# Block products for nine pairs of expert tiles in the second half of the V product

## The chip, the cores and the metric

The kernel runs on one core of one Trainium2 chip. Its time is the device time of one launch in microseconds (us); it is given as the median of several runs. One execution was taken with the hardware profiler, and every duration below comes from that execution.

## The reference

The kernel computes two transformer blocks in a row for 256 tokens of width 2048 in float32. The last step of the second block is a mixture of 16384 small experts (`peer_ffn`), and it is the only part that the change touches:

```
u = u_emb[expert]
a = jax.nn.gelu(jnp.einsum('thkd,td->thk', u, xb), approximate=False)
coef = (g * a)
return jnp.einsum('thk,thkd->td', coef, v_emb[expert])
```

`expert` holds 8 x 16 chosen experts for each token, and `g` their softmax weights. The result is added to the residual stream, and a last rmsnorm with the gain `g_final` gives the output, 256 x 2048.

## The kernel before

**Dense form.** Instead of gathering experts, the kernel makes a dense table of coefficients, 16384 experts x 256 tokens, zero where a token did not choose an expert. It lies in SBUF as `G`, 128 tiles of 128 experts x 256 tokens. The result is then a plain matrix product: for each expert tile j, coefficients (128 x 256 tokens) times rows of V (128 experts x 2048 columns), summed over j.

**Three products for one.** A float32 operand is split into a high part (`wh`, the value rounded to the narrow format fp32r) and a low part (`wl`, the remainder). TensorE computes high x high, high x low and low x high; that is `three` (lines 941 to 943). So one block product is three matmuls of 128 x 512.

**Two halves.** V is worked through twice: first columns 0 to 1023 for all 128 tiles ("first half"), then columns 1024 to 2047 ("second half"). One tile of a half is one chunk of 128 x 1024 floats, 512 KB. For each chunk `v_part_of` runs four block products (2 token blocks x 2 column blocks of 512), 12 matmuls, into four PSUM banks that accumulate over j: banks `ps4` to `ps7` in the first half and `ps0` to `ps3` in the second (`acc`).

**The engines around one chunk.** All chunks of the program stand in one list, `PLAN`.
- SP loads chunk i into one of four raw buffers (`load`, line 842), once VectorE has finished with chunk i-4 (semaphore `lo`). SP also issues every other DMA, in program order.
- ScalarE makes the high part (`cut`, line 2273), once TensorE has finished chunk i-3, and the high part of the coefficients of the next tile (`coef_high`, line 2655) into one of two buffers, once TensorE has finished the tile that used that buffer.
- VectorE makes the low parts (`coef_low`, line 2189, which counts the semaphore `c_l`; `cut`, line 1481, which counts `lo`).
- In the loop over j of the second half, ScalarE runs in turn `coef_high` for tile j+1 and `cut` for tile j+2, and VectorE runs `coef_low` for tile j+1 and `cut` for tile j+2, while TensorE works on tile j. "Step j" below means that turn.

**Other work in the second half.** The residual stream was parked in DRAM (`spill`). As tiles of `G` are used up, their space takes the residual (`fin`) and the gain (`gain`), in twelve pieces of 256 KB (`PIECE`, lines 918 and 920). Before piece n SP waits until `c_l` says that the tiles under it have been read (`c_l` at least 128 + 2n + 2, that is, the coefficients of tile 2n+1), and each stands in SP's order ahead of the load of tile 10 + 2n. At steps 50 to 62 VectorE adds the finished first half to the residual (`add_up`, line 2207), ScalarE squares it (line 2671) and VectorE multiplies by the gain (line 2236). After the last matmul the second half is added, the norm is taken and the output is stored.

Of the kernel before, what the change touches and what calls it, by code (L numbers as in the profile page):

```python
# [16 lines left out]
D = 2048  # L17
# [143 lines left out]
PLAN += [("V", j, c) for c in range(2) for j in range(128)]  # L161
# [333 lines left out]
def build(nc, A, out):  # L495
# [184 lines left out]
    fin = flatG[:, 0:2 * D].rearrange("p (q d) -> p q d", q=2)  # L680
# [26 lines left out]
    def pc(name, i=0):  # L707
# [53 lines left out]
        new(n) for n in ("v_part", "f_add", "f_sq", "f_ms", "f_rt", "f_rs", "f_out", "f_outv")]  # L761
    block = top.enter_context(nc.Block())
# [74 lines left out]
    def _(y):  # L837
# [42 lines left out]
        for i in range(RN, NCH):  # L880
# [58 lines left out]
    def _(t):  # L939
# [495 lines left out]

        def v_last():
# [16 lines left out]
        for i in range(U0, NCH):  # L1453
            name, j, c = PLAN[i]
            if name == "U":
                if c == 0:
                    if j < 4:
                        t.wait_ge(qp_ok, 5 + j)
                    else:
                        t.wait_ge(ev_u, j - 3)  # L1460
                chunk(i, u_place(j), 8 * c, 8, x4, c == 0, c == 1)
            elif (j, c) == (125, 1):
                v_last()
            elif c == 0 or j < 125:
                v_tile(j, c)
# [6 lines left out]
    def _(v):  # L1472
# [731 lines left out]
        def add_up(half, qt, b):  # L2204
            i = 2 * half + b
            x = fin[:, qt, 512 * i:512 * i + 512]
            v.tensor_tensor(x, x, acc(half, qt, b)[:], ALU.add).then_inc(f_add, 1)

        for j in range(128):
            if j < 125:  # L2210
# [12 lines left out]
            else:  # L2223
                cut(V1 + j + 2)
            if j in ADD_AT:
                n = ADD_AT.index(j)
                if n == 0:
                    v.wait_ge(d_re, 16 * 8)
                add_up(0, n // 2, n % 2)
            if j - 2 in ADD_AT:  # L2230
                n = ADD_AT.index(j - 2)
                if n == 0:
                    v.wait_ge(d_gf, 16 * 4)
                x = fin[:, n // 2, 512 * (n % 2):512 * (n % 2) + 512]
                v.wait_ge(f_sq, n + 1)
                v.tensor_tensor(x, x, gain[:, 512 * (n % 2):512 * (n % 2) + 512], ALU.mult).then_inc(own.up(), 1)
        for qt in range(2):
            for b in range(2):
# [18 lines left out]
            for c in (CH, CH + 512):  # L2257
                y = fin[:, qt, c:c + 512]
# [4 lines left out]
    def _(s):  # L2263
# [661 lines left out]
```

## Time and profile before

| | |
|---|---|
| median of 3 runs | 3174.89 us (3174.85 to 3175.99) |
| profiled execution | 3175.95 us |
| its span, first to last instruction | 3174.1 us |
| TensorE busy | 3160.3 us |
| VectorE busy | 2096.0 us (66%) |
| ScalarE busy | 1804.0 us (57%) |
| DMA, mean over the span | 198 GB/s |

Busy times are sums of the durations of instructions. Matmuls are pipelined and overlap in the records: one is shown as 389 ns although the next starts sooner. How long a piece of TensorE work takes is therefore read from start to start. On VectorE and ScalarE, too, an instruction may start a little before the record of the one ahead of it ends. The granted clock of TensorE is given as a share of full speed: 1.00 is 2.4 GHz, 0.50 is 1.2 GHz.

### The profile page before, as it was taken

To read this page: it belongs to the slowest core of one execution; us is meant where nothing else is said; L and a number is where in the kernel's file an instruction comes from. 1 tells how busy PE (TensorE), PEld (TensorE's weight loads), DVE (VectorE), ACT (ScalarE), POOL (GpSimd) and SP (SyncE) were. 2 spreads that over 40 slices of the span, in tenths; PEclk is the share of its full clock that TensorE was granted. 3 is DMA by queue.
4 is the path that set the end of the run, shared out by engine and by line. 5 is a ranking of instruction groups with operands and counts; after the bars stand their busy time and mean duration, and the time that the engine had idled before them with its cause. 6 is when DMAs were issued, how large, how long until landed. Compare 5 with 4: busy or idle time off the path is not lost.

```text
span 3174.1 us, 58774 instructions
## 1 busy us (share of the span) xinstructions
PE 3160.3 (100%) x24186; PEld 3018.3 (95%) x24186; DVE 2096.0 (66%) x3389; ACT 1804.0 (57%) x2580; POOL 458.0 (14%) x321
## 2 busy tenths in 40 slices
PE   9999999999999999999999999999999999999998
PEld 9999999999999999999999999999999888888887
DVE  7987486666664477665666699855555666666665
ACT  6566464444444455545455578877777544555545
POOL 0001200000000000000000056777760000000000
PEclk9999999999999999999999999999999999999999
DMA  6444557666666656545565577888876777766555
GB/s 224 151 146 134 183 181 235 225 226 229 226 201 194 194 172 206 163 153 166 187 196 197 199 190 194 196 195 195 194 195 196 243 242 242 242 226 216 195 194 168
DMA packets 229419, 627.77 MB, mean 198 GB/s; under 512 B 59328, under 2 KB 78624, under 8 KB 229024
## 3 DMA queue, kind: packets, MB, share of 16 engines
q1 hardware_dynamic: 192144, 623.60, 60.7%
q0 software_dynamic: 36864, 0.15, 3.3%
q8 instruction: 192, 3.15, 0.4%
q14 instruction: 75, 0.61, 0.1%
q10 hardware_dynamic: 144, 0.26, 0.0%
HBM read 601.27 MB, written 21.10 MB: 196 GB/s over the span
## 4 chain that ended last, share of the span: by engine, by line
PE 98%; DVE 1%; ACT 0%; DMA 0%; issue 0%; POOL 0%; SPq 0%; DVEq 0%; ACTq 0%; POOLq 0%
PE ps L941 32%; PE ps L942 31%; PE ps L943 31%; PE ps L1014 0%; DVE wl L1481 0%; PE ps L1215 0%; PE ps L1238 0%; PE ps L1235 0%; PE ps L982 0%; DMA raw<-in_in1k 0%; PE ps L1411 0%; PE ps L1249 0%; PE ps L1239 0%; PE ps L1067 0%; PE ps L1016 0%
## 5 line engine op out<-in xcount | busy, mean ns | idle before, releaser
L2273 ACT CAST wh<-raw 128x1024 fp32r<-128x1024 f32 (+3 forms) x1114 | 1158.2, 1040 | 1029.7 <-PE ps L943 1008.4
L1481 DVE TENSOR_TENSOR wl<-raw,wh 128x1024 fp32r<-128x1024 f32 (+2 forms) x883 | 1061.8, 1203 | 407.8 <-ACT wh L2273 405.4
L941 PE MATMUL ps<-xh,wh 128*128 128x256 f32 x3088 | 854.7, 277 | 0.5 <-issue 0.5
L943 PE MATMUL ps<-xh,wl 128*128 128x256 f32 x3088 | 850.0, 275 | 0.0
L942 PE MATMUL ps<-xl,wh 128*128 128x256 f32 x3088 | 849.8, 275 | 0.0
L941 PE MATMUL ps<-xw,wh 128*128 128x258 f32 (+2 forms) x2096 | 591.7, 282 | 2.8 <-DVE wl L1542 1.7
L943 PE MATMUL ps<-xw,wl 128*128 128x258 f32 (+2 forms) x2096 | 587.6, 280 | 0.0
L941 PEld LDWEIGHTS ps<-xh,wh 128*128 128x128 f32 x3088 | 579.7, 188 | 4.3 <-issue 1.6
L942 PEld LDWEIGHTS ps<-xl,wh 128*128 128x128 f32 x3088 | 579.8, 188 | 1.1 <-issue 1.0
L943 PEld LDWEIGHTS ps<-xh,wl 128*128 128x128 f32 x3088 | 579.6, 188 | 0.0
L2784 POOL DMA_INDIRECT table<-w_loose x256 | 397.6, 1553 | 809.3 <-DVE w_loose L2161 656.3
L1481 DVE TENSOR_TENSOR wl<-raw,ph 128x1024 fp32r<-128x1024 f32 x231 | 281.2, 1220 | 224.4 <-ACT ph L2278 187.7
L942 PE MATMUL ps<-xw,wh 128*128 128x258 f32 (+2 forms) x1441 | 404.2, 281 | 0.0
L941 PEld LDWEIGHTS ps<-xw,wh 128*128 128x128 f32 x2096 | 394.3, 188 | 5.4 <-DVE wl L1542 2.1
L943 PE MATMUL ps<-wh,coefs 128*128 128x512 f32 x1020 | 396.8, 389 | 0.0
L941 PE MATMUL ps<-wh,coefs 128*128 128x512 f32 x1020 | 396.8, 389 | 0.0
L942 PE MATMUL ps<-wl,coefs 128*128 128x512 f32 x1020 | 396.8, 389 | 0.0
L943 PEld LDWEIGHTS ps<-xw,wl 128*128 128x128 f32 x2096 | 394.0, 188 | 0.0
L942 PEld LDWEIGHTS ps<-xw,wh 128*128 128x128 f32 x1441 | 270.8, 188 | 0.1
L2278 ACT CAST ph<-raw 128x1024 fp32r<-128x1024 f32 x231 | 232.7, 1007 | 0.0
L941 PEld LDWEIGHTS ps<-wh,coefs 128*128 128x128 f32 x1020 | 191.4, 188 | 39.8
L943 PEld LDWEIGHTS ps<-wh,coefs 128*128 128x128 f32 x1020 | 191.4, 188 | 39.8
(398 smaller groups left out, 4454.7 us busy)
## 6 DMA issues: line engine op xcount, KB each, us to landing
raw<-in_peer_u SPq DMA_DIRECT2D x256, 512.0 KB
raw<-in_peer_v SPq DMA_DIRECT2D x256, 512.0 KB
raw<-in_w_in SPq DMA_DIRECT2D x172, 512.0 KB
raw<-in_w_up SPq DMA_DIRECT2D x82, 512.0 KB
raw<-in_w_gate SPq DMA_DIRECT2D x80, 512.0 KB
raw<-in_w_down SPq DMA_DIRECT2D x80, 512.0 KB
raw<-in_w_out SPq DMA_DIRECT2D x64, 512.0 KB
table<-tmp SPq DMA_DIRECT2D x32, 512.0 KB, 6.4
```

Source lines behind the costliest of these rows:

```text
L941: t.matmul(o, lh, rh, start=start, stop=False)
L942: t.matmul(o, lh, rl, start=False, stop=False)
L943: return t.matmul(o, ll, rh, start=False, stop=stop)
L1481: v.tensor_tensor(part_at(wl, i), raw[:, i % RN, 0:cols(i)], high.bitcast(F32), ALU.subtract).then_inc(lo, 1)
L2273: last = s.copy(part_at(wh, i), raw[:, i % RN, 0:cols(i)])
L2278: last = s.copy(ph[:, 2 + i % 2, :], raw[:, i % RN, 0:cols(i)])
L2784: g.indirect_dma_start(out=table, out_offset=bass.IndirectOffsetOnAxis(ap=eidx[q][:, n:n + 1], axis=0), in_=wts[q][:, n:n + 1], in_offset= ...
```

## The change

Nine pairs of neighbouring tiles, (26, 27), (36, 37), ... (106, 107), are taken out of the normal course of the second half. For a pair the product is a 2 x 2 by 2 x 2 product of blocks (2 token blocks, 2 expert tiles, 2 column blocks), and Strassen's scheme gives it with seven block products in place of eight, some of them of sums of blocks.

- **TensorE** (`v_pair`): seven products of three matmuls for a pair instead of eight. They go to seven banks: three of the usual four (`ps0`, `ps1`, `ps2`) and `ps4` to `ps7`, which must be free by then. So the first half is added to the residual at steps 11 to 14 now, no longer at 50 to 62.
- **VectorE and ScalarE** (`pair_step`): in the eight steps ahead of a pair, eight sums on VectorE (four of 128 x 512, four of 128 x 128), then the high part of 4096 columns on ScalarE and the low part on VectorE, in five pieces each. The two `cut`s of the pair's tiles fall away. A new pair's sums begin when TensorE has finished the pair before.
- **SP**: a pair's two raw tiles are loaded by two DMAs of 512 KB of their own (line 961 of the changed kernel) into the space of `G` under the old `fin`, ahead of the load that is named in `PAIR_LOAD`. For the first pair that is the load of tile 20; for the others it is the load of the first tile behind the pair before (tile 28, 38, ...), and SP first waits until VectorE has made the second low piece of the pair before (`pair_lo`), because that piece reads the same space.
- **Pieces**: the twelve pieces of residual and gain now stand ahead of the loads of tiles 8, 10, 12, 14 (residual, first half), 109 to 112 (residual, second half) and 18, 20, 22, 24 (gain). Their numbers n, and with them the count of `c_l` that SP waits for, are 0 to 3, 4 to 7 and 8 to 11 in that order.
- **Fold**: behind the last pair one copy and eight adds of 128 x 512 bring `ps4` to `ps7` into the residual, at steps 108 to 116.

```diff
+PAIRS = [26 + 10 * n for n in range(9)]
+PAIRED = [j + e for j in PAIRS for e in range(2)]
+SINGLE = [j for j in range(128) if j not in PAIRED]
+PLAN += [("V", j, 0) for j in range(128)] + [("V", j, 1) for j in SINGLE]
...
-PIECE = {AT["V", 10 + 2 * n, 1]: n for n in range(12)}
-
-ADD_AT = [50 + 4 * n for n in range(4)]
+PIECE = {AT["V", j, 1]: n for n, j in enumerate((8, 10, 12, 14, 109, 110, 111, 112, 18, 20, 22, 24))}
+
+ADD_AT = [11, 12, 13, 14]
+SQUARE_AT, GAIN_AT = [54, 64, 74, 84], [55, 65, 75, 85]
+
+
+BETWEEN = PAIRS[1] - PAIRS[0] - 2
+PAIR_LOAD = {AT["V", 20, 1]: 0}
+PAIR_LOAD.update({AT["V", j - BETWEEN, 1] + 8: n + 1 for n, j in enumerate(PAIRS[:-1])})
+BEHIND_PAIR = {j - BETWEEN + o: (n, o) for n, j in enumerate(PAIRS) for o in range(BETWEEN)}
+FOLD = {PAIRS[-1] + 3 + n: n for n in range(8)}
...
+    def fin_at(qt, c, n=512):
+        o = 2 * CH * (c // CH) + CH * qt + c % CH
+        return flatG[:, o:o + n]
+    pair_high, pair_low = [x[:, PAD_X[3]:PAD_X[3] + KT * S] for x in xbuf]
+    pair_raw = x_loose[:, 1, PAD_X[3]:PAD_X[3] + KT * S]
+    B11, B21, B22, T1_, T3_, T2_, T4_, SUMS = range(8)
+    RAW11, RAW12, RAW21, RAW22 = [flatG[:, 2 * CH + 512 * n:2 * CH + 512 * n + 512] for n in range(4)]
+    RAW_ROWS = flatG[:, 3 * CH:4 * CH]
+    folded = flatG[:, 3 * D + 3 * CH:3 * D + 3 * CH + 512]
...
                 y.wait_ge(c_l, 128 + 2 * n + 2)
                 c = slice(512 * (n % 4), 512 * (n % 4) + 512)
+                if n == 4:
+                    y.wait_ge(pair_lo, PAIR_LO + 5 * (len(PAIRS) - 1) + 2)
                 if n < 8:
-                    y.dma_start(fin[:, n // 4, c], spill[:, n // 4, c]).then_inc(d_re, 16)
+                    qt, x = n // 2 % 2, CH * (n // 4) + 512 * (n % 2)
+                    y.dma_start(fin_at(qt, x), spill[:, qt, x:x + 512]).then_inc(d_re if n < 4 else d_gf, 16)
                 else:
                     y.dma_start(gain[:, c], A["g_final"][:, c]).then_inc(d_gf, 16)
+            if i in PAIR_LOAD:
+                n = PAIR_LOAD[i]
+                if n:
+                    y.wait_ge(pair_lo, PAIR_LO + 5 * (n - 1) + 2)
+                else:
+                    y.wait_ge(c_l, 128 + 16)
+                for e in range(2):
+                    j = PAIRS[n] + e
+                    y.dma_start(flatG[:, (2 + e) * CH:(3 + e) * CH], A["peer_v_2"][128 * j:128 * j + 128, CH:2 * CH]).then_inc(d_pair, 16)
             load(i)
...
+        def v_pair(n):
...
+            t.wait_ge(pair_lo, PAIR_LO + 5 * (n + 1))
+            t.wait_ge(c_l, one + 1)
+            product(ps[4], single(one, 0), B11, first, last)
+            product(ps[5], summed(0), T1_, first, last)
+            t.wait_ge(c_l, two + 1)
+            product(acc(1, 0, 0), single(two, 0), B21, False, False)
+            product(acc(1, 1, 0), single(two, 1), T4_, False, False).then_inc(pair_mm, 1)
+            product(acc(1, 0, 1), summed(3), B22, False, False)
+            product(ps[6], summed(1), T2_, first, last)
+            product(ps[7], summed(2), T3_, first, last).then_inc(pair_mm, 1)
...
+                if c and j - 2 in PAIRS:
+                    v_pair(PAIRS.index(j - 2))
                 v_tile(j, c)
...
+            done = PAIR_SUM + 8 * n
+            if o == 0:
+                if n:
+                    v.wait_ge(pair_mm, PAIR_MM + 2 * n)
+                v.wait_ge(d_pair, D_PAIR + 32 * (n + 1))
+                v.tensor_tensor(t1, RAW12, RAW11, ALU.subtract).then_inc(pair_sum, 1)
+                v.tensor_tensor(t3, RAW22, RAW12, ALU.subtract).then_inc(pair_sum, 1)
+                v.tensor_tensor(sums[0], a21, a22, ALU.add).then_inc(pair_sum, 1)
+                v.wait_ge(pair_sum, done + 1)
+                v.tensor_tensor(t2, RAW22, t1, ALU.subtract).then_inc(pair_sum, 1)
+            elif o == 1:
+                v.wait_ge(pair_sum, done + 3)
+                v.tensor_tensor(sums[1], sums[0], a11, ALU.subtract).then_inc(pair_sum, 1)
+                v.wait_ge(pair_sum, done + 4)
+                v.tensor_tensor(t4, RAW21, t2, ALU.subtract).then_inc(pair_sum, 1)
+            elif o == 2:
+                v.tensor_tensor(sums[2], a11, a21, ALU.subtract).then_inc(pair_sum, 1)
+                v.wait_ge(pair_sum, done + 5)
+                v.tensor_tensor(sums[3], a12, sums[1], ALU.subtract).then_inc(pair_sum, 1)
+            if 2 <= o < 7:
+                pair_low_of(n, o - 2)
+
+        def pair_low_of(n, q):
+            x, y = ((0, 512), (512, 1536), (1536, 2560), (2560, 3584), (3584, 4096))[q]
+            whole_ = RAW11 if q == 0 else RAW_ROWS if q == 1 else pair_raw[:, x:y]
+            v.wait_ge(pair_hi, PAIR_HI + 5 * n + q + 1)
+            v.tensor_tensor(pair_low[:, x:y], whole_, pair_high[:, x:y].bitcast(F32), ALU.subtract).then_inc(pair_lo, 1)
...
+            steps = [(folded, ps[4]), (fin_at(0, CH + 512), folded), (fin_at(0, CH + 512), ps[5]), (folded, ps[7]),
+                     (fin_at(1, CH), folded), (fin_at(1, CH + 512), folded), (fin_at(1, CH + 512), ps[5]), (fin_at(0, CH), ps[4])]
...
+            if j in PAIRS:
+                coef_low(128 + j + 1)
+                cut(AT["V", j + 2, 1] + 2)
+                continue
...
+            elif n >= 130 and n - 130 in PAIRED:
+                s.wait_ge(pair_mm, PAIR_MM + 2 * (PAIRED.index(n - 130) // 2) + 1)
...
+        def pair_step(n, o):
+            if o > 4:
+                return
+            x, y = ((0, 512), (512, 1536), (1536, 2560), (2560, 3584), (3584, 4096))[o]
+            whole_ = RAW11 if o == 0 else RAW_ROWS if o == 1 else pair_raw[:, x:y]
+            if o == 0:
+                if n:
+                    s.wait_ge(pair_mm, PAIR_MM + 2 * n)
+                s.wait_ge(d_pair, D_PAIR + 32 * (n + 1))
+            elif o > 1:
+                s.wait_ge(pair_sum, PAIR_SUM + 8 * n + (2, 6, 8)[o - 2])
+            s.copy(pair_high[:, x:y], whole_).then_inc(pair_hi, 1)
```

**SP, second half of V, the loads of tiles 14 to 30.** `raw<-in_peer_v` is a chunk's load, `G<-spill` and `G<-in_g_final` are pieces of residual and gain, `G<-in_peer_v` is a raw tile of a pair; `s_c_l`, `s_lo` are the semaphores that SP waits for. Before:

```order
L842 DMA raw<-in_peer_v_2 128x1024 [waits s_lo] x2
L918 DMA G<-spill 128x512 [waits s_c_l]
L842 DMA raw<-in_peer_v_2 128x1024 [waits s_lo] x2
L918 DMA G<-spill 128x512 [waits s_c_l]
L842 DMA raw<-in_peer_v_2 128x1024 [waits s_lo] x2
L918 DMA G<-spill 128x512 [waits s_c_l]
```

And after:

```order
L871 DMA raw<-in_peer_v_2 128x1024 [waits s_lo] x4
L952 DMA G<-in_g_final 128x512 [waits s_c_l]
L871 DMA raw<-in_peer_v_2 128x1024 [waits s_lo] x2
L952 DMA G<-in_g_final 128x512 [waits s_c_l]
L961 DMA G<-in_peer_v_2 128x1024 [waits s_c_l]
L961 DMA G<-in_peer_v_2 128x1024
L871 DMA raw<-in_peer_v_2 128x1024 [waits s_lo] x2
L952 DMA G<-in_g_final 128x512 [waits s_c_l]
L871 DMA raw<-in_peer_v_2 128x1024 [waits s_lo] x2
L952 DMA G<-in_g_final 128x512 [waits s_c_l]
L871 DMA raw<-in_peer_v_2 128x1024 [waits s_lo] x2
L961 DMA G<-in_peer_v_2 128x1024 [waits s_cv_l]
```

The gain's four pieces, which stood ahead of tiles 26 to 32, stand ahead of tiles 18, 20, 22 and 24, each with a wait for `c_l`, and the first pair's raw tiles stand between the second of them and the load of tile 20.

**VectorE, steps 18 to 20 of the second half.** `coefs` is the low part of coefficients, `wl` that of a chunk, `x_loose` the place of a pair's sums, `xl` and `xh` a pair's low and high part. Before:

```order
L2189 TENSOR_TENSOR coefs<-G,coefs 128x256 [waits s_c_h]
L1481 TENSOR_TENSOR wl<-raw,wh 128x1024 [waits s_hi]
L2189 TENSOR_TENSOR coefs<-G,coefs 128x256 [waits s_c_h]
L1481 TENSOR_TENSOR wl<-raw,wh 128x1024 [waits s_hi]
L2189 TENSOR_TENSOR coefs<-G,coefs 128x256 [waits s_c_h]
```

And after:

```order
L1552 TENSOR_TENSOR wl<-raw,wh 128x1024 [waits s_hi]
L2290 TENSOR_TENSOR x_loose<-G 128x512 [waits s_d_km]
L2291 TENSOR_TENSOR x_loose<-G 128x512
L2292 TENSOR_TENSOR x_loose<-G 128x128
L2294 TENSOR_TENSOR x_loose<-G,x_loose 128x512 [waits s_cv_add]
L2260 TENSOR_TENSOR coefs<-G,coefs 128x256 [waits s_c_h]
L1552 TENSOR_TENSOR wl<-raw,wh 128x1024 [waits s_hi]
L2297 TENSOR_TENSOR x_loose<-x_loose,G 128x128 [waits s_cv_add]
L2299 TENSOR_TENSOR x_loose<-G,x_loose 128x512 [waits s_cv_add]
L2260 TENSOR_TENSOR coefs<-G,coefs 128x256 [waits s_c_h]
```

Four sums now stand between the `cut` of step 18 and the coefficients of tile 20, and two between the `cut` of step 19 and the coefficients of tile 21.

## Rows read from the trace of the kernel before

**Rows 1.** The page: engines, and the chain that ended last by engine.

```profile
PE 3160.3 (100%) x24186; PEld 3018.3 (95%) x24186; DVE 2096.0 (66%) x3389; ACT 1804.0 (57%) x2580; POOL 458.0 (14%) x321
...
PE 98%; DVE 1%; ACT 0%; DMA 0%; issue 0%; POOL 0%; SPq 0%; DVEq 0%; ACTq 0%; POOLq 0%
```

**Rows 2.** Waits, 2900 to 3100 us: engine line waited for, us, times, longest.

```profile
ACT coefs L2655 <- PE ps L943: 96.7, 73, 1.4
DVE wl L1481 <- ACT wh L2273: 39.1, 74, 0.5
DVE coefs L2189 <- ACT coefs L2655: 35.7, 66, 0.5
```

**Rows 3.** Timeline around one tile's start: start, us, engine, line, operation.

```profile
3002.16 0.39 PE L943 MATMUL ps<-wh,coefs 128*128 128x512 f32 x1
3002.38 0.39 PE L941 MATMUL ps<-wh,coefs 128*128 128x512 f32 x1
3002.58 0.41 ACT L2655 CAST coefs<-G 128x256 fp32r<-128x256 f32 x1 [1.36 <-PE ps L943]
3002.89 1.05 ACT L2273 CAST wh<-raw 128x1024 fp32r<-128x1024 f32 x1
3003.02 0.42 DVE L2189 TENSOR_TENSOR coefs<-G,coefs 128x256 fp32r<-128x256 f32 x1 [0.54 <-ACT coefs L2655]
3003.97 1.23 DVE L1481 TENSOR_TENSOR wl<-raw,wh 128x1024 fp32r<-128x1024 f32 x1 [0.53 <-ACT wh L2273]
3005.30 0.41 ACT L2655 CAST coefs<-G 128x256 fp32r<-128x256 f32 x1 [1.36 <-PE ps L943]
```

**Rows 4.** Timeline of VectorE with an add behind a cut, and of ScalarE near the end.

```profile
2955.01 1.23 DVE L1481 TENSOR_TENSOR wl<-raw,wh 128x1024 fp32r<-128x1024 f32 x1 [0.53 <-ACT wh L2273]
2956.16 0.68 DVE L2207 TENSOR_TENSOR G<-G,ps 128x512 f32<-128x512 f32 x1
2956.78 0.43 DVE L2189 TENSOR_TENSOR coefs<-G,coefs 128x256 fp32r<-128x256 f32 x1
...
3157.93 0.62 ACT L2683 CAST wh<-raw 128x512 fp32r<-128x512 f32 x1
3158.46 0.61 ACT L2684 CAST wh<-raw 128x512 fp32r<-128x512 f32 x1
```

**Rows 5.** Timeline of SP's queue, tiles 10 to 18 of the second half.

```profile
2831.15 3.05 SPq L842 DMA_DIRECT2D raw<-in_peer_v  x2
2834.24 0.43 SPq L918 DMA_DIRECT2D G<-spill  x1
...
2852.91 3.05 SPq L842 DMA_DIRECT2D raw<-in_peer_v  x2
```

**Rows 6.** Transfers of 256 KB: line 920 alone, and the page's DMA issues.

```profile
L920 SPq DMA_DIRECT2D G<-in_g_final x4: 432/432/432, 2872.3 to 2888.6; - x4
...
DMA to landing us min/median/max: 4.4/4.9/5.4
...
out<-G SPq DMA_DIRECT2D x7, 256.0 KB, 2.7
```

**Rows 7.** Stretches: busy us of PE, PEld, DVE, ACT, POOL; PEclk, DMA share, GB/s.

```profile
2999.79:3000.79 1.00, 1.00 (x6) 0.81 (x5) 0.43 (x1) 0.93 (x2) 0.00 (x0) 1.00 0.38 115
3000.79:3003.19 2.40, 2.40 (x12) 2.00 (x11) 1.40 (x2) 1.04 (x3) 0.00 (x0) 1.00 0.58 203
3003.19:3003.39 0.20, 0.20 (x3) 0.16 (x2) 0.20 (x1) 0.20 (x1) 0.00 (x0) 1.00 0.15 61
10.00:24.00 14.00, 13.96 (x112) 13.96 (x113) 11.49 (x17) 12.06 (x20) 2.02 (x7) 1.00 1.01 382
```

**Rows 8.** Timeline: the last matmul of the program.

```profile
3165.55 0.40 PE L943 MATMUL ps<-wh,xl 128*128 128x512 f32 x1
```

**Rows 9.** Stretches behind the last matmul.

```profile
3167.00:3168.00 1.00, 0.00 (x0) 0.00 (x0) 0.30 (x2) 0.64 (x4) 0.00 (x0) 1.00 1.05 352
3168.00:3168.50 0.50, 0.00 (x0) 0.00 (x0) 0.20 (x3) 0.22 (x2) 0.00 (x0) 0.83 0.96 336
3168.50:3169.00 0.50, 0.00 (x0) 0.00 (x0) 0.50 (x1) 0.50 (x1) 0.00 (x0) 0.50 0.13 45
```

**Rows 10.** Waits of TensorE over the whole span, the longest kinds.

```profile
PE ps L941 <- DVE wl L1542: 1.7, 2, 1.2
PE ps L941 <- issue: 1.6, 2, 1.1
```

More of the change, by code:

```diff
@@ L1434, in v_tile, with product, single, summed @@
             last.then_inc(gemm, 1)
+        def v_pair(n):
+            j = PAIRS[n]
+            one, two = 128 + j, 128 + j + 1
+            first, last = n == 0, n == len(PAIRS) - 1
+            def product(o, left, b, start, stop):
+                return three(o[:], *left, pair_block(pair_high, b), pair_block(pair_low, b), start, stop)
+            def single(tile, qt):
+                tk = slice(128 * qt, 128 * qt + 128)
+                return coef_at(0, tile)[:, tk], coef_at(1, tile)[:, tk]
+            def summed(i):
+                return pair_sum_at(pair_high, i), pair_sum_at(pair_low, i)
+            if first:
+                t.wait_ge(f_add, 4)
+            t.wait_ge(pair_lo, PAIR_LO + 5 * (n + 1))
[8 more added lines that the diff above has]
+            product(ps[7], summed(2), T3_, first, last).then_inc(pair_mm, 1)
         def v_last():
@@ new lines, in pair_low_of, with fold @@
+        def pair_low_of(n, q):
[3 more added lines that the diff above has]
+            v.tensor_tensor(pair_low[:, x:y], whole_, pair_high[:, x:y].bitcast(F32), ALU.subtract).then_inc(pair_lo, 1)
+        def fold(n):
+            steps = [(folded, ps[4]), (fin_at(0, CH + 512), folded), (fin_at(0, CH + 512), ps[5]), (folded, ps[7]),
+                     (fin_at(1, CH), folded), (fin_at(1, CH + 512), folded), (fin_at(1, CH + 512), ps[5]), (fin_at(0, CH), ps[4])]
+            x, y = steps[n]
+            if n == 0:
+                v.wait_ge(pair_hi, PAIR_HI + 5 * len(PAIRS) + 1)
+                v.wait_ge(d_gf, 16 * 8)
+            else:
+                v.wait_ge(pair_sum, PAIR_SUM + 8 * len(PAIRS) + n)
+            v.tensor_tensor(x, x, y if y is folded else y[:], ALU.add).then_inc(pair_sum, 1)
@@ L2222, in _ @@
                 last.then_inc(lo, 1)
-            else:
-                cut(V1 + j + 2)
+            elif j in SINGLE and j - 2 not in PAIRS:
+                cut(AT["V", j, 1] + 2)
+            if j in BEHIND_PAIR:
+                pair_step(*BEHIND_PAIR[j])
+            if j in FOLD:
+                fold(FOLD[j])
             if j in ADD_AT:
@@ L2684, in _ @@
                 s.copy(part_at(wh, i)[:, 512:CH], raw[:, i % RN, 512:CH]).then_inc(hi, 1)
-            else:
+            elif j in SINGLE and j - 2 not in PAIRS:
                 cut(AT["V", j, 1] + 2)
-            if j - 1 in ADD_AT:
-                n = ADD_AT.index(j - 1)
+            if j in BEHIND_PAIR:
+                pair_step(*BEHIND_PAIR[j])
+            if j == PAIRS[-1] + 2:
+                s.wait_ge(pair_mm, PAIR_MM + 2 * len(PAIRS))
+                s.copy(folded, ps[6][:]).then_inc(pair_hi, 1)
+            if j in SQUARE_AT:
+                n = SQUARE_AT.index(j)
                 square_up(0, n // 2, n % 2)
@@ L2708, in _ @@
                 s.wait_ge(f_out, 4)
-                s.dma_start(out[128:256, 512:1024], fin[:, 1, 512:1024]).then_inc(d_out, 16)
+                s.dma_start(out[128:256, 512:1024], fin_at(1, 512)).then_inc(d_out, 16)
     @block.gpsimd
```

39 lines of the change are left out of this document (26 added, 13 removed).

## The prediction

> **What bounds the kernel now.** I read the page first, then the waits, then the timeline of one tile, then SP's queue and the transfers. The page shows TensorE busy for the whole span and 98% of the chain on it [rows 1]; over the whole span its longest wait is 1.2 us [rows 10]. In the second half of V every other engine waits: ScalarE 1.36 us in each tile for TensorE, VectorE twice 0.54 us for ScalarE [rows 2, 3]. So a matmul taken away is time gained, as long as nothing makes TensorE wait; and a delay elsewhere costs only what exceeds its slack.
>
> A tile takes 2.72 us (3002.58 to 3005.30) and is 12 matmuls, 0.227 us each [rows 3]. From its start (3002.38) its ScalarE copy begins after 0.20 us, and the low coefficients for the next tile are ready after 1.06 us (3003.44).
>
> What an instruction takes of its engine, start to start: on VectorE a 1024-column cut 1.15 us (2955.01 to 2956.16), a 512-column add 0.62 [rows 4], coefficients 0.34 (0.43 less the overlap of 0.09 seen on the others); a 128-column sum I extrapolate from 0.43 at 256 and 0.68 at 512 columns to 0.29, so 0.2 start to start. On ScalarE coefficients 0.31 [rows 3], 512 columns 0.53 [rows 4], 1024 columns 1.05 less 0.09, 0.96.
>
> **Part 1, the matmuls removed.** Nine pairs, three matmuls less in each: 27 x 0.227 = 6.1 us saved. It is the same form (128 x 512) from other buffers, so I take the same 0.227.
>
> **Part 2, the work added on VectorE and ScalarE.** In ten tiles, now 8 x 2.72 + 21 x 0.227 = 26.5 us of TensorE, VectorE has 10 coefficients (3.4), 8 cuts (9.2), six instructions of 512 columns (3.7), three of 1024 (3.4) and four small ones (0.8): 20.5 us, 77%. ScalarE has 3.1 + 7.7 + 1.1 + 2.9 = 14.8 us. Both fit in the mean. What hides this work is VectorE's idle time of 2 x 0.54 us a tile [rows 3]; without the overlap of 0.09 us on 31 instructions it would be 23.3 us, still less than 26.5. I cost it at nothing in the course between pairs. The fold's nine instructions (8 x 0.62 us on VectorE, one a step) fall in steps with 1.1 us of idle time and without pair work: nothing, at most 5 us if none were hidden. The adds of the first half come earlier; their four pieces are ordered six steps ahead. Nothing. The end of the kernel is unchanged.
>
> **Part 3, SP's queue from tile 18 to 25.** This is the term that decides. Before, the piece ahead of tile 18's load had n = 4 and asked for the coefficients of tile 9; the load was out at 2852.91 [rows 5], step 13 of this half. Now the piece there has n = 8, so SP waits for c_l = 128 + 18, the coefficients of **tile 17**, which VectorE makes in step 16. In the same step ScalarE wants tile 18's raw data. Behind the waiting instruction stand the load of tile 18, that of tile 19, and the next piece, which wants tile 19's coefficients, and so on four times (tiles 18, 20, 22, 24). The four loads in advance shrink to none.
>
> Price of a landing: a 512 KB load issued at 2999.79 moves little before 3000.79 and is mostly done by 3003.39, 3.6 us after issue [rows 7]; 256 KB take 2.7 us alone, and 4.9 us behind a 512 KB load that was issued 0.4 us earlier [rows 6]. Under a full queue 382 GB/s are moved [rows 7], 1.37 us for 512 KB. From the first and second I take 2.3 us + 1.45 us for each 512 KB queued in one burst; bounds are 2.0 + 1.3 (2.7 us less 0.7; the full queue) and 3.1 + 1.6 (5.3 us from the load's issue for 768 KB, less 1.5 units; 3.6 us less 2.0).
>
> The chain, in us from the start of tile 16:
> - Coefficients 17 at 1.06, SP issues gain and load 18 (1.5 units, 4.5 us): landed 5.6. ScalarE high part to 6.65, VectorE low part 7.9, coefficients 18 behind it 8.2, tile 18 starts at 8.3. It was due at 5.44: **2.9 late**.
> - Load 19 lands at 7.0, its high part is done at 8.1 and its low part at 9.4; coefficients 19 at 9.7. Now gain, the pair's 1 MB and load 20 go out together, 3.5 units, 7.4 us: landed 17.1. High part 18.2, low part 19.4, four sums 3 x 0.62 + 0.2 ahead of coefficients 20, which end at 21.85. Tile 20 starts at 21.9, while tile 19 ended at 13.75: **8.2 late**.
> - Low part 21 (1.15), two sums (0.8), coefficients 21 at 24.15. Gain and load 22, 4.5 us: 28.65. High 29.75, low 31.0, two small sums and a piece of 512 columns 1.0, coefficients 22 at 32.35. Tile 22 at 32.45, due 27.4: **5.1 late**.
> - Low part 23, a pair piece of 1024 columns (both 1.15), coefficients 23 at 35.0. Load 24 landed 39.5, high 40.55, low 41.8, pair piece 1.15, coefficients 24 at 43.3. Tile 24 at 43.4, due 37.9: **5.5 late**.
>
> Sum 21.7 us. With the lower bounds it is 19.2, with the upper 26.1, by the same chain.
>
> **Part 4, a pair's raw tiles ahead of a load.** For the other pairs SP waits for the second low piece of the pair before. In us from the start of the first tile behind a pair: that piece comes in the fourth step and ends at 12.1. The pair's two tiles and the load of the first tile behind the pair are 3 units, 2.3 + 4.35: landed 18.8. ScalarE wants it in the seventh step, at 16.8. So its high part is done at 19.85, its low part at 21.1, then the last low piece of the pair (0.68) at 21.7 and the pair's coefficients at 22.1; the pair is due at 21.76. 0.4 late, and 0.12 at the pair's second tile: 0.52 x 7 = 3.6 us (the pair at 26 falls in part 3, the one at 106 has no load in its way). By the bounds it is nothing (landed 17.9) or 1.8 each, 13 us.
>
> **Part 5, the clock.** The last matmul starts at 3165.55 [rows 8], the granted clock is still 1.00 up to 3168.0 and 0.50 from 3168.5 on, which is 1.2 GHz [rows 9]. The stalls of 8.2, 5.1 and 5.5 us are longer than that gap. At half speed a matmul costs 0.2 us more. The first two slow starts hide in the next stall, where ScalarE's and SP's chain decides; only the last one counts. How fast the clock comes back no row of before shows: between nothing and one whole tile (2.4 us); I take the middle, 1.2.
>
> The Trainium skill (TensorE: Matmul & The Clock Gate, section "HAM oscillation — how this bites in real kernels") says that a kernel whose matmuls stop for each DMA wait starts each batch at the low clock. The trace agrees as far as it can, with the fall to 0.50 behind the last matmul. By that rule part 5 would be above nothing, and without it nothing.
>
> **The sum.** 21.7 + 3.6 + 1.2 - 6.1 = 20.4 us. The profiled execution took 3175.95 us (span 3174.1), so it would take 3196.4; the median of the runs is 1.1 lower: **3195 us**.
>
> On the price of a landing the Trainium skill (DMA: Bandwidth & Descriptors, section "Anatomy of one DMA — SWDGE (gpsimd) path") fits 2.0 us + bytes / 436 GB/s for another issuing path. That would be 1.2 us for each 512 KB, and the sum by it, an estimate, some 12 us slower than before. The rows here show more (3.6 us for one load, 382 GB/s), and I keep to them.
>
> **Rivals.**
> - *Quick landings.* The lower bounds in parts 3 and 4: 19.2 + 0 + 1.2 - 6.1 = +14.3 us, 3189. For it speaks 382 GB/s under load; against it the 4.9 us of a gain piece behind one load.
> - *Slow landings, and pairs that wait each time.* The upper bounds: 26.1 + 13 + 1.2 - 6.1 = +34, 3209. For it speaks that at 1000 columns a step VectorE has little room in the steps with pair pieces, so that part 4's delay is not made up; against it that a single load is done in 3.6 us.
> - *SP's wait stays covered (the other side).* Then only the 27 matmuls count: 3168.8, or up to 3172 with part 4. It would decide if the load of tile 18 landed before 3.0 us in the chain above, so that its low part were ready at 5.4: within 1.9 us of its issue. The shortest 256 KB transfer, 2.7 us [rows 6], speaks against it. For it speaks only that none of the twelve piece waits of before delayed anything, but there the tile asked for was nine tiles ahead of the load behind it, and now it is one.
> - *VectorE as the bound of the whole half*: were its instructions not to overlap and the waits for its own results to add 0.1 us each, the steps with pair pieces would take some 3 us instead of 2.72, 1.5 us a pair at most, 13 us. It is held by the upper end.
>
> **How the numbers follow.** My forecast (between +17 and +27 us) 0.55; quick landings 0.17; slow landings or VectorE 0.21; covered wait 0.06; anything else 0.01. A measurement of this kernel can tell 0.2%, 6.3 us, from no change; the covered wait ends just inside it, at -6.1, and by a little more or less on either side of it: 0.02 of its 0.06 for faster, 0.04 for the same, and another 0.01 for the same from what is not thought of. So faster 0.02, same 0.05, slower 0.93. The range, 3185 to 3211, takes in both landing bounds.
>
> **What would show it.** Right: in the profile after, TensorE waits four times near tiles 18, 20, 22 and 24, the second time longest, some 22 us in all, for coefficients or cuts whose ScalarE copy waited for a DMA; the granted clock falls there; SP's loads of 18 to 25 come in twos. Then 27 matmuls fewer, and 0 to 1 us of waiting ahead of each pair. Wrong: no wait of TensorE ahead of tile 18 (then the load did not hang on the coefficients of tile 17), a matmul of a pair that takes more than 0.227 us, or VectorE without idle time from tile 28 on.

## The result

The changed kernel takes 3209.09 us (median of 4 runs, 3208.24 to 3210.67) against 3174.88 us: the ratio is 1.0107, 95% interval 1.009 to 1.0125, that is 34.2 us slower. The forecast was 3195 us in a range of 3185 to 3211. The time is in the range and near its upper end, so the sum was 14 us too small.

### The profile page after: what moved, and what is told of

The parts are those of the page before. It is cut to its first block, busy times and chain, and to the rows that moved or that the text cites. A ratio compares the mean times of both kernels' runs of the same rounds, so it can differ in the third digit from the quotient of the medians.

```text
span 3206.4 us, 58846 instructions
## 1 busy us (share of the span) xinstructions
PE 3172.4 (99%) x24159; PEld 3018.8 (94%) x24159; DVE 2142.9 (67%) x3496; ACT 1821.8 (57%) x2608; POOL 459.2 (14%) x321
## 4 chain that ended last, share of the span: by engine, by line
PE 95%; DVE 2%; DMA 2%; ACT 1%; issue 0%; SPq 0%; POOL 0%; DVEq 0%; ACTq 0%; POOLq 0%
PE ps L982 31%; PE ps L983 30%; PE ps L984 30%; DMA raw<-in_peer_v 1%; DVE wl L1552 1%; PE ps L1055 0%; ACT wh L2397 0%; DVE xl L2311 0%; PE ps L1256 0%; PE ps L1279 0%; PE ps L1276 0%; PE ps L1023 0%; PE ps L1452 0%; DVE coefs L2260 0%; PE ps L1290 0%
## 5 line engine op out<-in xcount | busy, mean ns | idle before, releaser
L2397 ACT CAST wh<-raw 128x1024 fp32r<-128x1024 f32 (+3 forms) x1096 | 1138.9, 1039 | 1074.7 <-PE ps L984 1014.6
L1552 DVE TENSOR_TENSOR wl<-raw,wh 128x1024 fp32r<-128x1024 f32 (+2 forms) x865 | 1039.8, 1203 | 415.8 <-ACT wh L2397 411.5
L982 PE MATMUL ps<-wh,coefs 128*128 128x512 f32 x948 | 375.1, 396 | 18.8 <-DVE coefs L2260 18.8
L983 PE MATMUL ps<-wl,coefs 128*128 128x512 f32 x948 | 373.5, 394 | 0.0
L984 PE MATMUL ps<-wh,coefs 128*128 128x512 f32 x948 | 373.4, 394 | 0.0
L982 PEld LDWEIGHTS ps<-wh,coefs 128*128 128x128 f32 x948 | 179.8, 190 | 58.8 <-issue 16.2
L984 PEld LDWEIGHTS ps<-wh,coefs 128*128 128x128 f32 x948 | 180.8, 191 | 39.9
```

Of the source, the lines that this page charges most:

```text
L982: t.matmul(o, lh, rh, start=start, stop=False)
L983: t.matmul(o, lh, rl, start=False, stop=False)
L984: return t.matmul(o, ll, rh, start=False, stop=stop)
L1552: v.tensor_tensor(part_at(wl, i), raw[:, i % RN, 0:cols(i)], high.bitcast(F32), ALU.subtract).then_inc(lo, 1)
L2397: last = s.copy(part_at(wh, i), raw[:, i % RN, 0:cols(i)])
```

## The profile after

The page of the changed kernel, to be held against [rows 1]:

```profile
PE 3172.4 (99%) x24159; PEld 3018.8 (94%) x24159; DVE 2142.9 (67%) x3496; ACT 1821.8 (57%) x2608; POOL 459.2 (14%) x321
...
PE 95%; DVE 2%; DMA 2%; ACT 1%; issue 0%; SPq 0%; POOL 0%; DVEq 0%; ACTq 0%; POOLq 0%
```

27 matmuls are gone (24186 to 24159). The chain, 98% TensorE before, now has VectorE, DMA and ScalarE in it. The waits of the second half (2810 to 3200 us), engine and line, what it waited for, us, times, longest:

```profile
ACT wh L2397 <- DMA raw<-in_peer_v: 45.8, 13, 9.4
...
PE ps L982 <- DVE coefs L2260: 20.2, 8, 6.6
```

[rows 2] had no wait for a DMA at all. SP's own waits, before (2830 to 2880 us) and after (2855 to 2905 us):

```profile
SPq L842 <- DVE wl L1481: 38.5, 18, 2.4
...
SPq L952 <- DVE coefs L2260: 42.5, 4, 12.3
```

Before, SP waited for a free raw buffer, 2.4 us at most; now it waits four times, up to 12.3 us, for VectorE's low coefficients, in front of the gain's pieces. SP's queue, to be held against [rows 5], start and us:

```profile
2861.70 0.33 SPq L952 DMA_DIRECT2D G<-in_g_final  x1
2862.07 0.91 SPq L871 DMA_DIRECT2D raw<-in_peer_v  x2
2871.41 0.33 SPq L952 DMA_DIRECT2D G<-in_g_final  x1
2871.78 0.91 SPq L961 DMA_DIRECT2D G<-in_peer_v  x2
2872.73 1.14 SPq L871 DMA_DIRECT2D raw<-in_peer_v  x2
2886.22 0.33 SPq L952 DMA_DIRECT2D G<-in_g_final  x1
2886.59 0.91 SPq L871 DMA_DIRECT2D raw<-in_peer_v  x2
2897.72 0.33 SPq L952 DMA_DIRECT2D G<-in_g_final  x1
```

The loads of tiles 18 to 25 go out in twos, each two behind a gain piece, 9.7, 14.8 and 11.5 us apart where two tiles take 5.4. Step 16 begins at 2860.6, and the first gain piece goes out 1.1 us later, as the prediction's chain has it. ScalarE, which wants those loads:

```profile
2867.27 1.04 ACT L2397 CAST wh<-raw 128x1024 fp32r<-128x1024 f32 x1 [6.06 <-DMA raw<-in_peer_v]
2879.27 1.04 ACT L2397 CAST wh<-raw 128x1024 fp32r<-128x1024 f32 x1 [9.40 <-DMA raw<-in_peer_v]
2891.44 1.05 ACT L2397 CAST wh<-raw 128x1024 fp32r<-128x1024 f32 x1 [8.10 <-DMA raw<-in_peer_v]
2903.48 1.04 ACT L2397 CAST wh<-raw 128x1024 fp32r<-128x1024 f32 x1 [7.54 <-DMA raw<-in_peer_v]
```

From the gain piece's issue to the cut that waits for the load behind it: 5.6, 7.9, 5.2 and 5.8 us, where I had 4.5, 7.4, 4.5 and 4.5. TensorE at tiles 18, 20, 22 and 24 (the time in brackets is the idle time behind the end of the record ahead):

```profile
2870.05 0.47 PE L982 MATMUL ps<-wh,coefs 128*128 128x512 f32 x1 [3.85 <-DVE coefs L2260]
2884.06 0.76 PE L982 MATMUL ps<-wh,coefs 128*128 128x512 f32 x1 [6.63 <-DVE coefs L2260]
2895.23 0.76 PE L982 MATMUL ps<-wh,coefs 128*128 128x512 f32 x1 [3.44 <-DVE coefs L2260]
2907.41 0.77 PE L982 MATMUL ps<-wh,coefs 128*128 128x512 f32 x1 [4.88 <-DVE coefs L2260]
```

Tile 24 was due 21.8 us behind 2860.6, at 2882.4, and starts at 2907.4: 25.0 us late. From stall to stall, with the slow clock in between, TensorE lost 4.0, 8.6, 5.7 and 6.7 us. The clock, in stretches cut at its changes (columns as in [rows 7]; the eighth number is the granted clock):

```profile
2871.16:2874.57 3.41, 3.41 (x10) 2.64 (x9) 0.22 (x1) 0.00 (x0) 0.00 (x0) 0.50 0.53 102
2874.57:2881.40 6.83, 2.86 (x13) 2.00 (x11) 1.05 (x1) 2.13 (x4) 0.00 (x0) 1.00 0.77 294
2881.40:2888.23 6.83, 4.17 (x10) 3.33 (x11) 4.79 (x10) 1.94 (x3) 0.00 (x0) 0.50 0.13 23
...
2905.29:2912.12 6.83, 4.71 (x11) 3.78 (x12) 6.31 (x8) 2.36 (x4) 0.00 (x0) 0.50 0.93 362
2912.12:2940.00 27.88, 27.88 (x121) 22.55 (x121) 19.61 (x29) 15.50 (x23) 0.00 (x0) 1.00 0.45 156
```

It fell to 0.50 (1.2 GHz) within or just behind each of the four stalls. The matmuls between 2907.41 and 2912.12 started 0.427 us apart, 0.2 more than at 2.4 GHz, and the first two 0.56: 2.3 us in all.

The last stretch holds what I had not expected: 121 matmuls in 27.88 us with the clock at 1.00 and no wait, 0.230 us each, not 0.227. On a long stretch, 190 us, of before:

```profile
2960.00:3150.00 190.00, 190.00 (x840) 157.34 (x839) 119.03 (x147) 96.78 (x147) 0.00 (x0) 1.00 0.59 194
```

and of after:

```profile
2960.00:3150.00 190.00, 188.36 (x801) 149.99 (x800) 143.84 (x210) 106.16 (x163) 0.00 (x0) 1.00 0.56 193
```

The waits at pairs and the slow matmuls behind them take 3.8 us of this stretch, 16 or 17 of the missing 39 matmuls; the others are missing without a wait. From start to start plain tiles' matmuls go every 0.2333 us up to 3191, and every 0.2267 before 2865. I call these the slower and the faster rhythm.

So the 32.3 us by which the span is longer (3206.4 against 3174.1), with the last matmul starting at 3197.7 and not 3165.5, are made of: tile 24 late 25.0; half clock behind it 2.3; pairs waiting, with slow first matmuls, 3.9; some 1180 matmuls x 0.0066 = 7.8; less 6.1 for the 27 matmuls. That is 32.9; tile 16 started 0.3 us earlier than before, and the last 30 matmuls, as the next lines show, were 0.2 us quicker.

The slower rhythm is in the kernel before too, at its very end. There a weight load (PEld) starts 0.05 us behind the matmul ahead of its own:

```profile
3158.55 0.39 PE L943 MATMUL ps<-wh,coefs 128*128 128x512 f32 x1
3158.60 0.19 PEld L941 LDWEIGHTS ps<-wh,coefs 128*128 128x128 f32 x1
3158.78 0.39 PE L941 MATMUL ps<-wh,coefs 128*128 128x512 f32 x1
```

Up to there matmuls start 0.2267 us apart, and the last 30 start 0.23 and soon 0.2333 us apart. In the changed kernel the same place, at 3191, turns 0.2333 into 0.2267.

## The experiments

**Taking the held queue away.** `a1_gain_later`:

```diff
-PIECE = {AT["V", j, 1]: n for n, j in enumerate((8, 10, 12, 14, 109, 110, 111, 112, 18, 20, 22, 24))}
+PIECE = {AT["V", j, 1]: n for n, j in enumerate((8, 10, 12, 14, 109, 110, 111, 112, 30, 32, 34, 40))}
```

> The changed kernel with one edit: the gain's four pieces stand ahead of the loads of tiles 30, 32, 34 and 40 instead of 18, 20, 22 and 24, so that the coefficients they ask for are long made. Theory A (SP's queue, held by those waits, made the stalls of 4.2, 7.0, 3.8 and 5.3 us): no wait of TensorE from tile 18 to 25 and no fall of the clock; the stalls of 0.3 to 0.5 us ahead of pairs stay, about 3 us in all. Rival R (the pair's work itself, on ScalarE and VectorE, makes them): stalls stay near tiles 20 to 24. On the second thing seen after the change, that a matmul starts every 0.233 us instead of 0.227 from tile 24 on: theory M (a weight load that came late once puts TensorE into the slower rhythm, and it stays there) expects 0.233 us from the first stall ahead of a pair on, so 3174.9 - 6.1 + 3 + about 7.5 = 3179 us. Rival C (the slower rhythm comes from the clock's fall and return) expects 0.227 throughout and 3172 us.

Measured: 3184.47 us, ratio 1.0025 (1.0015 to 1.0036). 24.6 us of the 34.2 are gone with the place of four small DMAs; no wait is left at tiles 18 to 25, the clock stays at 1.00, and rival R falls. The time is 5 us above the 3179 us of theory M: the waits at pairs, with the slow matmuls behind them, came to 8.8 us and not 3. The first of them (1.4 us late from start to start):

```profile
2889.69 0.47 PE L982 MATMUL ps<-xh,coefs 128*128 128x512 f32 x1 [1.25 <-DVE coefs L2260]
```

The slower rhythm is there though the clock never fell, so rival C falls too. It began at tile 20, where nothing waited.

**The pairs' raw tiles.** `a2_pair_loads_later` is a1 with

```diff
-PAIR_LOAD.update({AT["V", j - BETWEEN, 1] + 8: n + 1 for n, j in enumerate(PAIRS[:-1])})
+PAIR_LOAD.update({AT["V", j - BETWEEN, 1] + 10: n + 1 for n, j in enumerate(PAIRS[:-1])})
```

> As the one before, and each pair's two raw tiles (but the first pair's) are loaded two loads later, ahead of the third single tile behind the pair before instead of the first. Theory A with part 4 of the prediction (the pair's 1 MB delayed the load behind it): no wait of TensorE at all in the second half, and with theory M or C alike 0.227 us a matmul: 3174.9 - 6.1 = 3168.8 us. Rival V (VectorE's work ahead of a pair makes the small stalls): they stay, 3172 to 3179 us. Rival F (matmuls that read a pair's buffers are slower by themselves): 0.233 us in or behind pairs without any stall, 3170 to 3177 us.

Measured: 3176.87 us, ratio 1.0004 (0.9995 to 1.0014). TensorE waits nowhere in the second half: the pairs' waits hang on the place of their raw loads, as part 4 says, and rival V falls. But the time is 8 us above 3168.8; the rhythm is the slower one from tile 20 on, as in a1. The timeline of a2 there (PEld is the weight load, which the engine begins one matmul ahead):

```profile
2870.46 0.42 DVE L2260 TENSOR_TENSOR coefs<-G,coefs 128x256 fp32r<-128x256 f32 x1
...
2870.71 0.39 PE L983 MATMUL ps<-wl,coefs 128*128 128x512 f32 x1
2870.71 0.19 PEld L984 LDWEIGHTS ps<-wh,coefs 128*128 128x128 f32 x1
...
2870.93 0.40 PE L984 MATMUL ps<-wh,coefs 128*128 128x512 f32 x1
2871.00 0.19 PEld L982 LDWEIGHTS ps<-wh,coefs 128*128 128x128 f32 x1
2871.17 0.39 PE L982 MATMUL ps<-wh,coefs 128*128 128x512 f32 x1
```

Each weight load starts with the matmul ahead of its own, until the one of tile 20: it starts 0.07 us behind. VectorE's four sums of step 18 had pushed the coefficients to 2870.88, 0.29 us ahead of the tile's first matmul but too late for its load. That matmul still starts on time. From there on the rhythm is 0.2333 us.

**The held queue alone.** `b1_hold_only` is the kernel before with

```diff
-PIECE = {AT["V", 10 + 2 * n, 1]: n for n in range(12)}
+PIECE = {AT["V", j, 1]: n for n, j in enumerate((10, 12, 14, 16, 26, 28, 30, 32, 18, 20, 22, 24))}
```

> The kernel before with one edit: the gain's four pieces stand ahead of the loads of tiles 18, 20, 22 and 24, where the changed kernel has them, and the residual's second four take their former places. No pairs. Theory A: four stalls of TensorE of 3.5 to 4 us at tiles 18, 20, 22 and 24, about 15 us, about 1 to 2 us of matmuls at half clock. Theory M or C adds 0.0067 us x 12 x 100 tiles = 8 us of slower rhythm behind them: 3200 us. If the held queue costs only what the new 1 MB and the pair's sums add: under 3180 us.

Measured: 3200.27 us, ratio 1.008 (1.0063 to 1.0097). Its waits from 2860 to 2905 us:

```profile
ACT wh L2273 <- DMA raw<-in_peer_v: 26.8, 5, 7.7
...
PE ps L941 <- DVE coefs L2189: 11.6, 4, 3.9
```

Without a single pair the new order of eight small DMAs costs 25 us, four stalls and the slower rhythm behind them. A piece of the same size stood ahead of each of these four loads in the kernel before, without a stall: it is the wait that holds the queue, not the bytes.

**One late coefficient.** `b2_one_late` is the kernel before with, in VectorE's loop,

```diff
+            for n in range({20: 4}.get(j, 0)):
+                v.tensor_tensor(x_loose[:, 1, 512 * n:512 * n + 512], G[:, 110:112, :].rearrange("p a b -> p (a b)"),
+                                G[:, 112:114, :].rearrange("p a b -> p (a b)"), ALU.add)
             if j < 125:
                 coef_low(128 + j + 1)
```

> The kernel before, and at step 20 of the second half VectorE does four additional adds of 128 x 512 into an unused place ahead of the coefficients of tile 21, so that these are ready about 0.3 us after TensorE wants them. Nothing else is changed, and the clock has no cause to fall. Theory M: one late weight load puts the rhythm from 0.227 to 0.233 us for the rest, about 104 tiles x 0.08 = 8.3 us: 3183.5 us. Rival C (clock): a stall of 0.3 us and nothing more, 3175.2 us.

Measured: 3183.62 us, ratio 1.0021 (1.0012 to 1.0031). One stall of 0.27 us and what follows it make 8 us. Its long stretch has 24 matmuls fewer than that of before, with the clock at 1.00 and TensorE never idle:

```profile
2960.00:3150.00 190.00, 190.00 (x816) 154.16 (x815) 116.31 (x143) 94.39 (x144) 0.00 (x0) 1.00 0.54 188
```

Two of its ten runs took 3175.6 us: by their times, the same event does not always set off the slower rhythm.

**Two of them.** `b3_two_late` has `{20: 4, 60: 4}` in that line.

> As b2_one_late, with the four additional adds at step 20 and again at step 60. The first puts matmuls to 0.233 us. If a late weight load only ever puts the rhythm to the slower one (theory M as it stands): 0.233 us from tile 21 to the end, 3184 us. If each disturbance chooses anew, or toggles: 0.227 us again from tile 61 on in some or all runs, 40 tiles x 0.08 = 3.2 us and two stalls of 0.3 us: 3179 us.

Measured: 3183.66 us, ratio 1.0024 (1.0015 to 1.0034). Eight runs lie at 3183.3 to 3184.4 and two at 3180.7 and 3181.2. The second event mostly changes nothing; the two runs fit a return to 0.227 us for part of the way. The profiles of b1 and a5 (below) show such returns, b1 behind its second stall, at 2878.9, for two tiles; and in the changed kernel, b2, b3 and b5 the rhythm goes back to 0.2267 for the last 28 or 29 matmuls. So it is not a one-way switch.

**Late for the load only.** `b5_just_late` is b2 with three adds of 512 columns and one of 160.

> The kernel before, with three adds of 512 columns and one of 160 at step 20, about 0.36 us less than in b2_one_late, so that the coefficients of tile 21 are late for its weight load by less than 0.1 us but in time for its matmul. Theory M (lateness of the load alone): no idle time of TensorE, yet 0.233 us a matmul from there: 3183 us. Rival S (TensorE has to stop for the rhythm to change): 3174.9 us. As the margin is some hundredths of a microsecond, runs may fall on both sides.

Measured: 3183.07 us, ratio 1.002 (1.001 to 1.0029); two of ten runs at 3174.8 and 3175.4. The weight load of tile 21 starts 0.10 us behind the matmul ahead, and the matmul is on time:

```profile
2872.66 0.39 PE L943 MATMUL ps<-wh,coefs 128*128 128x512 f32 x1
2872.76 0.19 PEld L941 LDWEIGHTS ps<-wh,coefs 128*128 128x128 f32 x1
2872.89 0.39 PE L941 MATMUL ps<-wh,coefs 128*128 128x512 f32 x1
```

Rival S falls: 0.1 us of lateness that stops nothing costs 8 us in eight of the ten runs.

**The same work, not late.** `b6_same_work_not_late` does two of the adds at step 20 and two at step 24.

> The kernel before, with the four additional adds of b2_one_late in two parts, two at step 20 and two at step 24, so that no coefficient is late. Theory M: 0.227 us throughout and 3174.9 us. Rival W (additional work of VectorE, in whatever place, changes TensorE's rhythm): 3183 us.

Measured: 3175.12 us, ratio 1.0 (0.999 to 1.0009). No weight load is late but the one at 3158 that the kernel before has too, and rival W falls.

**The first pair's sums spread.** `a3_first_sums_split` is a2 with

```diff
                 v.tensor_tensor(sums[0], a21, a22, ALU.add).then_inc(pair_sum, 1)
-                v.wait_ge(pair_sum, done + 1)
-                v.tensor_tensor(t2, RAW22, t1, ALU.subtract).then_inc(pair_sum, 1)
+                if n:
+                    v.wait_ge(pair_sum, done + 1)
+                    v.tensor_tensor(t2, RAW22, t1, ALU.subtract).then_inc(pair_sum, 1)
             elif o == 1:
+                if n == 0:
+                    v.wait_ge(pair_sum, done + 1)
+                    v.tensor_tensor(t2, RAW22, t1, ALU.subtract).then_inc(pair_sum, 1)
```

> As a2_pair_loads_later, and for the first pair alone the fourth sum stands in step 19 instead of step 18, behind the coefficients of tile 20 and not ahead of them. In a2 these ended 0.28 us before tile 20 was due, its weight load started 0.06 us late, TensorE did not idle, and the slower rhythm began there. Theory M: no late weight load, 0.227 us a matmul throughout, 3174.9 - 6.1 = 3168.8 us. Rival F (the rhythm comes with a pair's own matmuls or with VectorE's higher load): 0.233 us from tile 26 or earlier, about 3176 us as a2. Rival V (the same work, only moved, makes another coefficient late a few steps on): 0.233 us from that step on, 3176 us.

Measured: 3176.63 us, ratio 1.0004 (0.9994 to 1.0014), so theory M by itself missed. No weight load is late up to tile 125, and the rhythm is 0.227 up to the first pair and 0.233 behind it. The matmuls on that border, PE alone:

```profile
2887.45 0.39 PE L984 MATMUL ps<-wh,coefs 128*128 128x512 f32 x1
2887.68 0.39 PE L982 MATMUL ps<-xh,coefs 128*128 128x512 f32 x1
2887.91 0.39 PE L983 MATMUL ps<-xl,coefs 128*128 128x512 f32 x1
2888.14 0.40 PE L984 MATMUL ps<-xh,coefs 128*128 128x512 f32 x1
...
2889.06 0.39 PE L982 MATMUL ps<-xh,coefs 128*128 128x512 f32 x1
2889.29 0.40 PE L983 MATMUL ps<-xl,coefs 128*128 128x512 f32 x1
2889.53 0.40 PE L984 MATMUL ps<-xh,coefs 128*128 128x512 f32 x1
```

The change of rhythm comes within the pair's first matmuls, with nothing to wait for and no late load; the seventh to ninth start 0.23 to 0.24 us apart, and the plain tiles behind the pair 0.2333. There is a second cause, in the pair's own matmuls.

**Where a pair's operands lie.** `a4_pair_offsets` is a3 with

```diff
-    pair_high, pair_low = [x[:, PAD_X[3]:PAD_X[3] + KT * S] for x in xbuf]
-    pair_raw = x_loose[:, 1, PAD_X[3]:PAD_X[3] + KT * S]
+    pair_high, pair_low = [x[:, 64:64 + KT * S + 4] for x in xbuf]
+    pair_raw = x_loose[:, 1, 64:64 + KT * S + 4]
...
-        return x[:, 512 * SUMS + 128 * n:512 * SUMS + 128 * n + 128]
+        return x[:, 512 * SUMS + 4 + 128 * n:512 * SUMS + 4 + 128 * n + 128]
```

and the last cut's columns moved by 4 with them. A matmul has two operands, the weights, which are loaded first, and the moving one; both are moved here, to the offsets that a plain tile's have.

> As a3_first_sums_split, in which no weight load was late and the slower rhythm began with the first pair's own matmuls. There the moving operand starts 28 floats into its buffer where a single tile's starts at 0, and the sums that serve as weights start at 28 as well, where a tile's coefficients start at 4. Here a pair's blocks start 64 floats in and its sums 4 floats behind a multiple of 64, so both stand to 64 as those of a single tile do; nothing else is changed. Theory O (the offsets of the two operands set off the slower rhythm): 0.227 us in the pairs and behind them, 3175.1 - 6.1 = 3169 us, a version faster than both. Rival F (seven banks, or weights from the same buffer as the moving operand): 0.233 us from the first pair on, 3176.6 us as a3.

Measured: **3168.95 us**, ratio 0.9984 (0.9975 to 0.9993), 6.3 us below the 3175.22 us of the kernel before: the 27 matmuls and nothing else. It is faster than both kernels, if only by 0.2% than the one before. The long stretch has 840 matmuls, as before the change:

```profile
2960.00:3150.00 190.00, 190.00 (x840) 157.34 (x839) 148.08 (x213) 108.26 (x166) 0.00 (x0) 1.00 0.56 193
```

Two of its eleven runs took 3176.9 and 3177.1 us; no profile shows these two, but the size is that of the slower rhythm.

**The offset alone, without pairs.** `b7_offset` is the kernel before with

```diff
-    return {"in1k": 24, "in1": 24, "out1": 20}.get(name, 26 if name == "gu" and m % 2 == 0 else 0)
+    return {"in1k": 24, "in1": 24, "out1": 20, "V": 28 * (PLAN[i][2] == 1)}.get(name, 26 if name == "gu" and m % 2 == 0 else 0)
```

and `part_at(wh, i)[:, dd]` for `wh[:, i % SN, dd]` in `v_part_of`.

> The kernel before, and the high and low parts of the second half's chunks start 28 floats into their buffers instead of at 0, so that every matmul of that half reads its moving operand at the offset that a pair's had. No pairs. Theory O: about 0.231 to 0.233 us a matmul in the whole second half (1536 matmuls x 0.004 to 0.0067 = 6 to 10 us), 3181 to 3185 us. Rival F: 3175.1 us.

Measured: 3185.55 us, ratio 1.0032 (1.002 to 1.0044). The rhythm is 0.233 us from the half's first tiles on, without a pair and without a late load. Rival F falls: the offset of the moving operand suffices.

**A pair's loads put back.** `a5_pair_loads_back` is a4 with `+ 8` in `PAIR_LOAD` again.

> As a4_pair_offsets, with each pair's raw tiles loaded where the change has them, two loads earlier. Part 4 of the prediction: each of the eight pairs from 26 to 96 has to wait about 0.5 us for its coefficients (a1 showed 0.3 to 1.9 us in the slower rhythm). Theory M adds that the first late weight load puts the rhythm to 0.233 us from there on, some 1150 matmuls, 7.7 us: about 3169 + 4 + 8 = 3181 us. Without M: 3173 us.

Measured: 3185.05 us, ratio 1.003 (1.0019 to 1.0041), 16 us above a4 and 4 us above what I expected: in the profiled run some 7 us of waits at pairs, with the slow matmuls behind them, in place of 4, and the slower rhythm behind most of them. In its profile the rhythm is 0.227 us for parts of the way (from about 2973 and from about 3060).

## Why the prediction was right, and where it was not

1. *The matmuls removed, 6.1 us*: right in count and price; a4 shows 6.3 us with nothing around it. The step's second sentence, "I take the same 0.227", is the one that failed.
2. *The added work on VectorE and ScalarE at nothing*: right for the mean, as a4 shows with VectorE busy 148 of 190 us. Wrong in one place: in step 18 the sums made tile 20's coefficients late for their weight load in a1 and a2. I had asked whether they are in time for the matmul, not for the load that starts 0.23 us sooner. In the changed kernel itself that place is hidden under the stalls.
3. *SP's held queue*: right in cause, place and order; b1 and a1 show it from both sides. b1 adds 24.9 us, of which some 8 are the slower rhythm; a1 takes away 24.6 us, although its waits at pairs are 5 us larger. Sized 21.7 us (2.9, 8.2, 5.1 and 5.5), measured 25.0 (4.0, 8.6, 5.7 and 6.7). The term that was too small is the landing: 4.5 us taken for 768 KB, 5.2 to 5.8 measured, two of the three above the upper bound of 5.5, and 7.9 against 7.4 for the long one. One more load stood in the queue behind each of these; whether it slows them no run shows. By the same chain, the estimate of "some 12 us" under the sum comes to 13.6.
4. *A pair's raw tiles ahead of a load*: right in cause; 3.6 us forecast, 3.9 measured, gone in a2. That the sums agree is in part luck: six pairs wait and not seven, five of them for 0.6 to 1.0 us and not 0.52, and mostly, some 0.5 us, at the pair's second tile, for which I had 0.12. In a1 and a5 the same loads cost 7 to 9 us; why more than in the changed kernel I have not tested.
5. *The clock*: 1.2 us forecast, 2.3 measured. It fell as that part said, and also behind the first stall of 4.0 us, which I had as 2.9. The rule of the Trainium skill (TensorE: Matmul & The Clock Gate, section "HAM oscillation — how this bites in real kernels") cited there is borne out by the four falls to 0.50, in a part that is small here.
6. *Not in the sum*: 0.0067 us more for each matmul from tile 24 on, 7.8 us. This, with 3.3 for landings, 1.1 for the clock and 0.3 for the pairs, makes the difference (12.5 of 13.8 us; the medians lie 34.2 us apart and the two profiled spans 32.3, which is the rest and a little more). The prediction named a matmul above 0.227 us as a sign of its being wrong, but gave it no price. In the changed kernel three things that set it off come together (stalls, the first sums, the pairs' offsets), and I have not taken them apart there; the pairs' offsets alone would have done it (a3), and so would the stalls (b1).

Without the slower rhythm the time would be some 3201 us, in the range as well; the 7.8 us took up room that its upper end had for slow landings and VectorE. The rival with slow landings forecast 3209 us, the measured time, and that is luck: its 26.1 us for the queue are near the 25.0 measured, but it put 13 us into waits at pairs, which cost 3.9, and the slower rhythm filled the gap.

## What to carry to other kernels

SP issued its DMAs in program order, so when a small transfer is moved, look up what its wait asks for and which loads stand behind it: here the wait went from nine tiles ahead of the load to one, and cost 25 us where the change could give 6. When TensorE is the bound, ask of each weight operand whether it is ready one matmul before it is needed (its load started that much earlier here), and give a new buffer the offset of the one that it replaces. And count matmuls in a long stretch against another kernel's: that shows a price per instruction that neither busy shares nor waits show.

## What the runs showed of the hardware

- The same 128 x 512 matmul runs in one of two rhythms at a granted clock of 1.00: 0.2267 or 0.2333 us from start to start (840 or 816 matmuls in 190 us). Which one holds can change at an event and then mostly stays, in b2 for over 1200 matmuls.
- A weight load 0.10 us late, with the matmul on time, sets off the slower one in most runs (eight of ten by their times in b5), and so does a stall of 0.27 us (eight of ten in b2); the profiles show the change at loads 0.05 us (before, 3158.6) and 0.07 us (a2) late as well. An event can also bring the faster one back: the place at the end that turned it slower in the kernel before turned it faster in the changed kernel, b2, b3 and b5, and changed nothing in a2, a3 and b1.
- With the moving operand 28 floats into its buffer and the weights 4 floats in, the slower one holds (b7); with 0 and 4 the faster one (before, a4). Why is open: no run tried offsets other than these and a3's (both at 28, slower), or moved the weights alone.
- The granted clock fell to 0.50 behind a stall of 4.0 us, 1.1 us after matmuls had begun again; it did not fall in a1, where matmuls ahead of pairs started up to 1.9 us behind the ones ahead of them.
